# One trunk layer on one core: the first two expert weight loads are held until the first position rows have landed, and three rows of the last stage are loaded behind the last expert

## The reference

```
x = x_sample + positions                       # latent tokens only
h = rms_norm(x) * (1 + sc1) + sh1
z = h @ w_in                                   # RWKV-7 both directions, conformer convolution
x = x + g1 * (concat(y_rwkv, y_conv) @ w_out)
h = rms_norm(x) * norm2_g * (1 + sc2) + sh2
x = x + g2 * moe(h)                            # 4 groups, top 1, then top 2 of its 8 experts
y = rms_norm(x) * final_norm_g
```

## Time and profile before

| | |
|---|---|
| median of 3 executions | 1175.06 us (1174.89 to 1177.2) |
| the profiled execution | 1173.66 us, of which the span of the profile is 1171.9 us |
| busy: TensorE, VectorE, ScalarE, GpSimd | 922.9, 598.4, 306.5, 63.4 us |
| moved by DMA | 193.76 MB, on average 165 GB/s |
| SyncE's DMA queue (q1) | 174.19 MB |
| ScalarE's DMA queue (q10) | 8.06 MB |

### The profile page before, as it was taken

The page is one execution under the profiler, slowest core; times in us unless marked ns, Lnnn a source line. Parts: engine busy times, 40 slices in busy tenths (PEclk is TensorE's granted clock), DMA queues, the critical chain, the costliest instruction groups (busy, mean ns, idle before and its releaser), DMA issues.

```text
span 1171.9 us, 15456 instructions
## 1 busy us (share of the span) xinstructions
PE 922.9 (79%) x5867; PEld 556.1 (47%) x5867; DVE 598.4 (51%) x1258; ACT 306.5 (26%) x522; POOL 63.4 (5%) x55
## 2 busy tenths in 40 slices
PE   1599999999698798877858958983599984978654
PEld 1265466566365675765747624442334332333221
DVE  2326952697988868787973434447411110111016
ACT  2240102502544434576322252110011110101002
POOL 0000000010001010010100000001111111110010
PEclk9989999999886555675765978995599997999777
DMA  9844741110101110011007068112889999799343
GB/s 321 277 172 180 274 156 37 43 56 20 19 2 28 19 51 11 10 28 19 9 21 229 1 234 305 37 54 75 333 352 420 420 419 406 306 417 418 150 163 121
DMA packets 72743, 193.76 MB, mean 165 GB/s; under 512 B 42309, under 2 KB 42815, under 8 KB 58463
## 3 DMA queue, kind: packets, MB, share of 16 engines
q1 hardware_dynamic: 64416, 174.19, 39.7%
q0 software_dynamic: 5472, 10.53, 2.5%
q10 hardware_dynamic: 2783, 8.06, 1.9%
HBM read 181.80 MB, written 19.34 MB: 172 GB/s over the span
## 4 chain that ended last, share of the span: by engine, by line
PE 46%; DVE 23%; DMA 16%; ACT 8%; issue 4%; SPq 1%; ACTq 1%; DVEq 0%; POOLq 0%; POOL 0%
PE bank L539 12%; DMA arena<-in_expert_w_up 8%; PE bank L2135 8%; PE bank L1547 4%; PE bank L2157 3%; DVE arena L1121 3%; DVE arena L1119 3%; PE bank L508 2%; DMA arena<-udiag 1%; DVE arena L975 1%; DVE arena L1072 1%; DVE arena L1003 1%; DMA udiag<-arena 1%; DMA arena<-winv 1%; PE bank L1237 1%
## 5 line engine op out<-in xcount | busy, mean ns | idle before, releaser
L539 PE MATMUL bank<-arena 128*128 128x320 f32 x704 | 203.7, 442 | 2.1 <-ACT arena L389 2.1
L539 PEld LDWEIGHTS bank<-arena 128*128 128x128 f32 x704 | 131.6, 192 | 75.0 <-issue 25.9
L2135 PE MATMUL bank<-arena 128*64 128x512 f32 (+2 forms) x528 | 132.0, 667 | 33.5 <-DMA arena<-in_expert_w_up 32.6
L975 DVE SCALAR_TENSOR_TENSOR arena<-arena 128x655 f32<-128x655 f32 x116 | 107.9, 930 | 4.2
L2135 PEld LDWEIGHTS bank<-arena 128*64 128x64 f32 (+2 forms) x528 | 46.7, 150 | 117.2 <-issue 115.9
L2215 DVE TENSOR_TENSOR arena<-arena,bank 128x256 f32<-128x256 f32 x17 | 7.2, 422 | 161.1 <-ACT arena L2189 161.1
L2157 PE MATMUL bank<-arena 128*64 128x512 f32 (+2 forms) x264 | 64.1, 627 | 10.0 <-DVE arena L2218 10.0
L1547 PE MATMUL bank<-arena 128*128 128x512 f32 x160 | 71.8, 607 | 0.0
L1547 PEld LDWEIGHTS bank<-arena 128*128 128x128 f32 x160 | 30.7, 194 | 37.8 <-issue 37.8
L2189 ACT ACTIVATE arena<-bank 128x256 f32<-128x256 f32 x17 | 6.5, 385 | 143.1 <-PE bank L2135 143.1
L1121 DVE TENSOR_TENSOR arena<-arena 128x56 f32<-128x56 f32 (+22 forms) x155 | 40.7, 263 | 5.3
(11 more groups left out here) (334 smaller groups left out, 1374.9 us busy)
## 6 DMA issues: line engine op xcount, KB each, us to landing
arena<-in_expert_w_gate SPq DMA_DIRECT2D x33, 1024.0 KB, 16.0
arena<-in_expert_w_up SPq DMA_DIRECT2D x33, 1024.0 KB, 20.3
arena<-in_expert_w_down SPq DMA_DIRECT2D x33, 1024.0 KB, 18.0
arena<-in_ada_w SPq DMA_DIRECT2D x12, 2048.0 KB, 9.4
arena<-in_w_in SPq DMA_DIRECT2D x22, 512.0 KB, 4.2
arena<-expert_rows SPq DMA_DIRECT2D x10, 512.0 KB, 7.4
arena<-in_x_sample SPq DMA_DIRECT2D x8, 512.0 KB, 5.8
arena<-in_w_out SPq DMA_DIRECT2D x1, 4096.0 KB, 15.0
```

Of the source, the lines that this page charges most:

```text
L539: mm = nc.tensor.matmul(psum[4 + 2 * (n % 2) + half][:, 0:HALF], wring[:, n % NWIN, k], hT[:, k, half * HALF:(half + 1) * HALF], start=(k ...
L975: chain(nc.vector.scalar_tensor_tensor(acc, src, w, acc, ALU.mult, ALU.add))
L2135: mm = nc.tensor.matmul(psum[2 + n % 2][r, :], xeT[:, n % 2, c, r], gu[:, :, c, :], start=(c == 0), stop=(c == KD - 1))
```

## The change

SyncE waits until the first position rows have landed (`s_pos2` at 16) before it issues the six loads of experts 0 and 16. The two loads of g2b leave the end of `sp_out`, and the load of fgain leaves its place behind the fourth expert; all three now stand behind the loads of the 32nd expert and ahead of the overflow round. No other engine's list is touched, and s_fg still counts to 48.

```diff
@@ sp_out @@
             sp.dma_start(rb[:, 0:4], ins["router_group_b"].broadcast_to([P, 4])).then_inc(s_rw, 16)
             sp.dma_start(rb[:, 4:36], ins["router_expert_b"].broadcast_to([P, 32])).then_inc(s_rw, 16)
-            for c in range(2):
-                sp.dma_start(g2b[:, c], modrows[c:c + 1, 5 * D:6 * D].broadcast_to([P, D])).then_inc(s_fg, 16)
@@ block.sync @@
             sp_out()
+            sp.wait_ge(s_pos2, 16)
             for n in range(2):
                 experts_load(n)
             sp.wait_ge(s_ids, 1)
             sp.wait_ge(s_h2st, 16 * TILES)
             for n in range(2, 4):
                 experts_load(n)
-            sp.dma_start(fgain, ins["final_norm_g"].rearrange("(o n) -> o n", o=1).broadcast_to([P, D])
-                         ).then_inc(s_fg, 16)
             sp.wait_ge(s_ovst, 1)
             for n in range(4, NEXP):
                 experts_load(n)
+            for c in range(2):
+                sp.dma_start(g2b[:, c], modrows[c:c + 1, 5 * D:6 * D].broadcast_to([P, D])).then_inc(s_fg, 16)
+            sp.dma_start(fgain, ins["final_norm_g"].rearrange("(o n) -> o n", o=1).broadcast_to([P, D])
+                         ).then_inc(s_fg, 16)
             sp_overflow()
             sp_end()
```

## The result

The changed kernel takes 1166.44 us in the median of 4 executions (1165.19 to 1167.6), against 1174.97 us before (1173.76 to 1177.2): a ratio of 0.9925, with a 95% interval of 0.9906 to 0.9944. It is faster, by 8.5 us in the medians and by 6.6 to 11 us in the interval. It was profiled in an execution of 1165.77 us with a span of 1164.1 us, 7.8 us shorter than before.

What follows compares the result with a forecast made beforehand. No engine bounds the whole kernel; PE holds 46% of the chain that ended last. Terms: -4.1 (stop) - 4.5 (clock) + 0 + 0 + 0 = -8.6 us, so 1166.5 us for a median, range 1163.5 to 1172.5.

Steps and rivals of the forecast that it cites:

- What delays the first rows: First position load, issued at 706.45: 8.49 us because of loads on SyncE's queue; with those away, 3.6 us.
- the sharing: At the first position load: it shares the full DMA with eight SyncE loads of 0.5 to 1.0 MB, taken as the cause.
- The first term, the stop: First turn: TensorE's wait for h2 from 722.27 to 726.39 goes, gaining 4.1 us.
- The second term, the clock: Between first and second turn: without the stop the clock stays at 1.00, distance 17.57 instead of 22.09, gaining 4.5 us.
- the rival that the clock falls anyway: Behind the first turn: the stop goes but a stretch at 0.50 remains; gain 4.1 us, 1171.0 us; chance 0.10.
- What is late next: Second position rows: they meet the end of the expert loads, land at 729.9, cost nothing, with 1.2 us of cover.
- The move of fgain: At the first gather, 833.97: fgain shared 0.2 us at most; zero to 0.2 us gained, zero taken.
- The move behind the last expert: Before the overflow round: 1.57 MB, 3.7 us, issue covered by 12 us; cost zero to 3.7 us, zero taken.
- The sum: Whole kernel: -4.1 - 4.5 + 0 + 0 + 0 = -8.6 us, 1166.5 us for a median; chance of this forecast 0.67.
- nothing: Rival at the first position load: slow for a reason of its own, gain zero, 1175.1 us; chance 0.07.
- the same: Outcome that measurement can't tell from no change, within about 0.2%, 2.4 us; chance 0.08.

Runs made afterwards that it cites:

- run with the rows early: Kernel before, with ScalarE issuing the first position load before the square of the prompt heads, nothing held or moved: 1165.19 us, ratio 0.9935.
- run with the hold only: Kernel before plus only the wait that holds the six loads of experts 0 and 16 until the first position rows land: 1165.99 us, ratio 0.9949.
- the stop filled: Kernel before, with four extra matmuls of unused result ahead of the first turn's wait for h2: 1171.41 us, ratio 0.9991.
- the changed kernel again: Changed kernel, unaltered, timed once more against the kernel before in the last comparison: 1167.54 us, ratio 0.9945.
- run with the gap filled: Changed kernel, with one extra unused matmul between transposes and router matmuls of each of the first four turns: 1162.35 us, ratio 0.9919.
- run held behind the second rows: Changed kernel, with the six expert loads held until the second position rows have landed (s_pos2 at 32): 1166.57 us, ratio 0.9945.
- with the gaps filled too: Changed kernel, with one unused matmul in each of the first four turns and six ahead of the last: 1161.41 us, ratio 0.9900.

## Why the prediction was right

**What delays the first rows.** Right: with the loads held, they are used 3.72 us after their issue (3.75 were said). The run with the rows early shows that their lateness is the whole cause, and the run with the hold only that g2b had no part to speak of: 0.7 us on the rows and nothing in the time. What was said too simply is the sharing: in the traces three matrices in front do as much as six, and one, issued 3.8 us ahead, does nothing.

**The first term, the stop.** Right: 4.1 us said, 4.28 found, and no idle time in front of the first turn.

**The second term, the clock.** The mechanism was right and the size was not. 4.5 us were said, from a first distance of 17.57; it measured 19.23, a gain of 2.86. The step that failed is "with no stop, the engine goes from a full stretch straight into a turn, as it does at 748.48, where the clock stays at 1.00". It can stay, but need not: the gap of 0.9 us in a turn brought a short stretch at 0.50 behind the first turn in every trace with a gap and no long stop, and behind another turn in two (the stop filled, and the changed kernel again). One such stretch costs 1.7 us. The run with the stop filled shows the term alone in its trace (2.8 us), and the run with the gap filled shows where the rest went (the distance is 17.54 us there). So the rival that the clock falls anyway was half true: it falls, for a third of the time.

The Trainium skill, "TensorE: Matmul & The Clock Gate", section "Part 1: The HAM clock gate", has the gate follow how busy the array has been, and the amount paid differ from run to run; the traces agree, with the short stretch behind the first turn in one execution of the changed kernel, and behind the first and the third in the other.

**What is late next.** Right: the second rows met the end of the weights and took 6.5 us to land, which put L1642 at 28.9 us from the 48 matmuls (729.9 + 0.1 was said, 28.5). The 17.2 us to landing in the earlier trace rows are those of the fifth expert load, issued at 705.98, and not of the sixth, for which the trace has no landing; so 723.8 for the end of the weights was a misreading. The windows have the DMA full to 724 (1.01) and 0.17 from 724 to 726, so the end is some tenths later, and nothing in the sum hangs on it. The next turn had 2.2 us of cover instead of 1.2. The run held behind the second rows shows the cost to be nothing.

**The move of fgain.** Said to be worth zero to 0.2 us; the gather took 4.55 us in place of 4.29. It took 4.15 in the second trace of the changed kernel, so the 0.3 us goes both ways and no gain or loss of this edit can be told.

**The move behind the last expert.** Right in the result, with one thing not foreseen: SyncE needed 6.2 us to issue the three, in place of 1.4. The cover of 12 us took that. The overflow expert landed 4.0 us later after its issue (3.7 were said), and TensorE did not wait for it.

**The sum.** 8.6 us were said. The median fell by 8.5 us, but that close a hit is luck: the clock's term was 1.6 us too large, and the scatter of executions made up for it. The trace shows 6.8 us. The second trace of the changed kernel has 5.45 at the routing, and the later comparison 5.7 in the medians. Of the 7.8 us between the first two spans, 1.0 lies ahead of the change. In the chances, 0.07 for nothing and the 0.02 moved to it give 0.09 for the same, where 0.08 was said.

## What to carry to other kernels

A prefetch that nobody waits for is not free while it runs: here 3 to 6 MB of weights, not wanted for over 100 us after they had landed, held up one load of 512 KB on which the next stage stood. Look for such a small load on the chain that ended last, and see which larger ones were issued just ahead of it; then either hold those, or issue the small one earlier, which is worth the same. And price a stop of TensorE with what comes behind it: the stop of 4.1 us cost 2.9 us more through the clock. Work of no use in the stop gave 2.8 us of that back in a trace, of which a stretch at the low clock one turn later took 1.7 again, and no gain was measured in the time; in the last turn, and with the gaps filled too, it was clear of the noise. Last, count from the last instruction ahead of the edit, and compare stage by stage: here a stage that the edit doesn't touch moved the end of the span by some 2 us.

## What the runs showed of the hardware that was not expected

- A wait of 0.9 us within a turn, between two groups of short matmuls, can bring the granted clock from 1.00 to 0.50 (2.4 to 1.2 GHz) for 3.4 us, at 1.7 us a time, behind one turn and not behind the next that looks the same. With the wait filled, the first four turns kept 1.00 in both traces that have it.
- A load of 512 KB on ScalarE's queue was used 3.7 to 3.8 us after its issue with none or one matrix of 1.05 MB in front on SyncE's queue (the one issued 3.8 us ahead), and 8.0 to 8.6 us after it with three or six.
- The Trainium skill, "DMA: Bandwidth & Descriptors", section "Queues, rings and completion order", has each DMA engine take turns between the queues that have work. An estimate from that rule, with turns of as many bytes in either queue, which the page does not state: 0.52 MB that share evenly with as much of the other queue need 1.2 us more than alone (0.52 MB at 424 GB/s), so 5 us in all. With three or six matrices in front the runs show 8.0 to 8.6, and the measurement decides.
- SyncE took 2.96 us to issue the two loads of g2b and 3.23 us for fgain when the queue was so long that g2b landed 20.0 and 22.9 us after its issue, against 0.91 and 0.45 us at their places before.
